# TensorE's expert loop with eight experts a turn in place of two

## The reference

```
logits = ht @ w_router + b_router
top_val, top_idx = lax.top_k(logits, 4)
gates = softmax(top_val)
# for each expert e and the tokens routed to it:
gu = x @ w_gate_up[e] + b_gate_up[e]            # 1024 -> 2048
gate = minimum(gu[:, :1024], 7.0); up = clip(gu[:, 1024:], -7.0, 7.0)
act = gate * sigmoid(1.702 * gate) * (up + 1)
y = act @ w_down[e] + b_down[e]                 # 1024 -> 1024, times the gate, summed per token
```

## Time and profile before

| what | value |
|---|---|
| median of 3 runs | 1282.84 us (1281.08 to 1282.91) |
| the profiled execution, its own time | 1281.37 us |
| its span, first to last instruction | 1279.6 us |
| PE busy | 1082.8 us (85%) |
| moved from memory | 457 MB, 357 GB/s over the span |
| mean granted TensorE clock | 0.911 of full speed |

### The profile page before, as it was taken

How to read it: one execution, slowest core, us unless ns; L and a number is a source line. 1 busy time by engine, 2 the same in 40 slices (tenths; PEclk the granted TensorE clock), 3 DMA queues, 4 the chain that set the end, 5 groups by cost and what they waited for, 6 DMA issues and landing times.

```text
span 1279.6 us, 28615 instructions
## 1 busy us (share of the span) xinstructions
PE 1082.8 (85%) x11083; PEld 516.1 (40%) x11084; DVE 306.7 (24%) x816; ACT 198.4 (16%) x444; POOL 111.9 (9%) x216
## 2 busy tenths in 40 slices
PE   3988999979997667766999999996769799969997
PEld 1776877735442111112444444441113244414443
DVE  0245344448221000001221122210001012212112
ACT  2330123332110000000111111110001011101112
POOL 8100002023010000000000010000000000000000
PEclk9998999989998786777999999997779799979999
DMA  9646334797999999999999989999999999999765
GB/s 349 227 164 225 106 130 173 284 303 271 386 422 422 422 422 422 422 422 422 422 422 422 422 344 423 422 422 422 422 422 422 422 422 422 422 422 422 308 265 212
DMA packets 81280, 457.27 MB, mean 357 GB/s; under 512 B 7054, under 2 KB 8176, under 8 KB 31936
## 3 DMA queue, kind: packets, MB, share of 16 engines
q1 hardware_dynamic: 74704, 417.91, 80.5%
q10 hardware_dynamic: 4976, 33.10, 6.3%
q0 software_dynamic: 1568, 5.80, 1.5%
HBM read 455.72 MB, written 1.07 MB: 357 GB/s over the span
## 4 chain that ended last, share of the span: by engine, by line
PE 48%; SPq 20%; DMA 18%; DVE 8%; issue 3%; ACT 2%; ACTq 1%; DVEq 0%
PE bank L1935 17%; SPq L366 15%; DMA raw<-in_w_gate_up 10%; PE bank L1948 9%; PE bank L1497 7%; DMA dn<-in_w_down 5%; SPq L370 4%; PE bank L1908 2%; DMA odd<-in_w_gate_up 2%; PE bank L1820 2%; PE bank L1957 2%; DMA raw<-in_w_ada 1%; DVE aT L1392 1%; PE bank L1462 1%; DVE gated L1377 1%
## 5 line engine op out<-in xcount | busy, mean ns | idle before, releaser
L1935 PE MATMUL bank<-raw,xT 128*32 128x512 f32 x1600 | 219.8, 680 | 82.3 <-DMA raw<-in_w_gate_up 70.3
L1935 PE MATMUL bank<-odd,xT 128*32 128x512 f32 x1664 | 213.2, 652 | 40.2 <-DMA odd<-in_w_gate_up 40.2
L1377 DVE TENSOR_TENSOR gated<-bank,bias_i 128x256 f32<-128x256 f32 x51 | 21.6, 424 | 614.4 <-PE bank L1957 614.4
L1935 PEld LDWEIGHTS bank<-raw,xT 128*32 128x32 f32 x1600 | 49.7, 115 | 237.1 <-DMA raw<-in_w_gate_up 142.2
L842 ACT ACTIVATE evg<-bank 128x512 f32<-128x512 f32 x51 | 30.5, 597 | 739.6 <-PE bank L1935 739.6
L580 POOL TENSOR_TENSOR gatehot<-onehot,gates 128x128 f32<-128x128 f32 x102 | 54.9, 557 | 881.2 <-PE bank L1924 869.5
L1935 PEld LDWEIGHTS bank<-odd,xT 128*32 128x32 f32 x1664 | 54.9, 113 | 181.8 <-issue 93.8
L1948 PE MATMUL bank<-raw,aT 128*32 128x256 f32 x2016 | 119.7, 380 | 9.4 <-DVE aT L1392 6.3
L1497 PE MATMUL bank<-hT,raw 128*128 128x256 f32 (+1 forms) x496 | 115.5, 392 | 2.2 <-ACT hT L633 2.2
L1497 PEld LDWEIGHTS bank<-hT,raw 128*128 128x128 f32 (+1 forms) x496 | 94.2, 193 | 21.3 <-issue 4.1
L1948 PEld LDWEIGHTS bank<-raw,aT 128*32 128x32 f32 x2016 | 62.4, 110 | 59.9 <-DVE aT L1392 16.3
(11 more groups left out here) (404 smaller groups left out, 852.3 us busy)
## 6 DMA issues: line engine op xcount, KB each, us to landing
raw<-in_w_gate_up SPq DMA_DIRECT2D x128, 1024.0 KB, 28.6
odd<-in_w_gate_up SPq DMA_DIRECT2D x128, 1024.0 KB, 26.5
raw<-in_w_down SPq DMA_DIRECT2D x49, 1024.0 KB, 27.3
dn<-in_w_down SPq DMA_DIRECT2D x48, 1024.0 KB, 28.7
raw<-in_w_down ACTq DMA_DIRECT2D x31, 1024.0 KB, 9.0
raw<-in_w_ada SPq DMA_DIRECT2D x12, 2048.0 KB, 9.1
raw<-in_w_in SPq DMA_DIRECT2D x7, 2048.0 KB, 12.8
raw<-in_w_out SPq DMA_DIRECT2D x2, 2048.0 KB, 9.2
```

The source lines that it names most:

```text
L1377: body.step("gate", tt(gated[:, :, :, :], turned[:, :, 0:2, :], bias_i[:, :, 0:2].unsqueeze(3).to_broadcast([P, 4, 2, CAP]), ALU.add))
L1935: g = mm(bank[0][j * CAP:(j + 1) * CAP, :], xT[:, u % 2, u // 2, :], gu_slab(u, p)[:, j * NC:(j + 1) * NC], start=u == 0, stop=u == KT - 1)
```

## The change

The outer loop has 4 turns in place of 16, and its body holds the code of eight experts in place of two. Parity and count of an expert are now worked out from its place n in the turn.

```diff
             pe.wait_ge(S("items_ready"), 4)
-            with pe.Fori(0, NE // 2) as q:
-                after = pe.value_load(first_item[0:1, bass.ds(2 * q, 1)], min_val=0, max_val=NI)
-                for p in range(2):
-                    e, first = 2 * q + p, after
+            with pe.Fori(0, NE // 8) as r:
+                after = pe.value_load(first_item[0:1, bass.ds(8 * r, 1)], min_val=0, max_val=NI)
+                for n in range(8):
+                    p, q = n % 2, 4 * r + n // 2
+                    e, first = 8 * r + n, after
                     after = pe.value_load(first_item[0:1, bass.ds(e + 1, 1)], min_val=0, max_val=NI)
                     with pe.Fori(first, after) as i:
```

## The result

The changed kernel takes 1291.74 us (median of 4 runs, 1289.89 to 1292.24) against 1282.53 for the kernel before (four runs, one more than in the table of the time before): ratio 1.0079, 95% interval 1.0063 to 1.0094. It is 9.2 us slower. The forecast was 1283.9 with a range up to 1290.5, so the time lies outside. In the profiled execution the span is 1290.3 us against 1279.6, 10.7 us more.

What follows compares the result with a forecast made beforehand. Transfers bound the kernel to 603 us and from 760 to 1180, TensorE between and at the end. -3.5 + 1.1 + 2.2 + 1.2 = +1.0 us gave 1282.4 profiled, 1283.9 as median; range 1278.8 to 1290.5.

Steps and rivals of the forecast that it cites:

- What bounds the kernel, and which edges count: Expert stage: transfers bound most, TensorE 603 to 758 us and the end; removed edges at experts 12, 14, 30 save 3.5 us.
- The code is fetched again in each turn: TensorE's outer loop: 2,800 instructions do not stay, so each turn fetches its 11 to 13 packets again; 65 to 75 packets.
- Hidden at experts 8 and 24, not at 16, with 1.3 us of margin: Three remaining turn edges: slab waits hide the stall at 8 and 24; at 16 it opens a 1.2 us transfer hole.
- I take 2.5: Jump back at the remaining turn edges: TensorE waits 2.5 us for a code packet, opening a 1.2 us hole at expert 16.
- rival 3: Jump at expert 16: a 5 us stall opens the hole by 3.7 us; +3.5 us in sum, 1286.3; chance 0.13.
- The packets on the DMA engines: 1.1 + 2.2 us, spread over 16: Full transfer stretches: refetched code delays the busiest engine 1.1 us a packet; 1.1 us in the first, 2.2 in the second.
- rival 2: Full transfer stretches: code packets share few DMA engines; +4.3 us, 1287.1 with eight, +9.8, 1292.6 with four; chance 0.27.

Runs made afterwards that it cites:

- the carried register: Two kernels, four and two experts a turn, next expert's first item number kept in a register instead of read; against the kernel before: 1279.27 and 1278.25 us.
- six a turn: Against the changed kernel, six experts in the loop body for 30 experts, the last two behind the loop: 1292.02 us, ratio 1.0084.
- moving the edges: Against the changed kernel, experts 0 and 1 before the loop and six behind, so turn edges stand at experts 10 and 18: 1283.49 us.
- sixteen a turn: Against the changed kernel, sixteen experts in the loop body, leaving one jump back, in front of expert 16: 1290.75 us, ratio 1.0065.

## Why the prediction was wrong

- *What bounds the kernel, and which edges count.* Right. The PE stretch lost 2.3 us for experts 12 and 14, and the end 1.2 us for expert 30. The removed edges in the long stretch gave nothing: it takes 425.5 us with two and with four experts a turn, and 425.4 us with the shorter edges of the carried register.
- *The code is fetched again in each turn.* Right: 69 packets, 65 to 75 foretold; six a turn shows that the limit lies between 1,400 and 2,100 instructions.
- *Hidden at experts 8 and 24, not at 16, with 1.3 us of margin.* Right: moving the edges showed that the place decides, and sixteen a turn that expert 16 is all of it.
- *"I take 2.5" for the stall.* This step failed. The jump was mis-sized. The edge idle grew by 7.29 - 1.12 = 6.2 us, beyond the 5 us of rival 3. A transfer's 1.9 us was no stand-in for a missed jump. The code packet itself is 1.1 us of it: the packet's record starts at 803.02, 3.9 us after the branch began to wait, and the branch ended 1.4 us after it. What fills the other 5 us no row names.
- *Left out altogether:* the clock behind the stall. 7.3 us of idle brought the granted clock to 0.51, and the next gate-up cost 9.46 - 7.07 = 2.4 us more. So TensorE was 8.6 us late at expert 16 against the 2.5 taken; less the 1.3 us of margin, that makes a hole of 7.3 us. The long stretch shows 7.1 us, against the 1.2 forecast.
- *The packets on the DMA engines: 1.1 + 2.2 us, spread over 16.* The mechanism was right, the size was off in the second term: 4.4 us, three packets on the busiest of about eight engines at some 1.5 us each in place of two at 1.1. That is rival 2 with its eight engines, which had 4.4 for this term; the equal figure is luck, since it took four packets at 1.1 us. The first stretch cost 1.0 us, close to the 1.1, but this is one pair of profiles: it takes 297.0 to 298.7 us in the five kernels that fetch 2 to 5 code packets in it and 298.6 to 300.2 in the seven others (15 to 17), so the term is some 1.3 us and not known to better than half a microsecond.
- The rivals 2 and 3 were priced one at a time, at +4.3 and +3.5. Both held at once, and rival 3 at twice its price. Put together with the measured sizes: -3.5 + 1.0 + 4.4 + 7.1 = +9.0, against 9.2 in the medians.

## What to carry to other kernels

When a loop body grows, count its instructions against what the trace shows to stay, and look at the queue that carries code: a body that fits fetches nothing after its first turn, one that doesn't pays twice, at the jump and on the DMA engines that carry data. A stall is worth what its place makes of it: ask how many microseconds of transfers are queued there, since the same 7 us of idle cost nothing at experts 8, 10, 18 and 24, 7 us at expert 16, and nearly 9 us, slow matmuls included, at expert 12. And when two dear cases have different causes, price them together as well as one by one.

## What the runs showed of the hardware

- A jump of TensorE's sequencer to code that was not kept left PE idle for 6.9 to 7.6 us in the kernels without the hint, against 1.1 us with the code kept. TensorE kept a loop of about 1,400 instructions and not one of about 2,100 (both counts are estimates from 350 for an expert).
- After 7.3 us of idle at expert 16 the granted clock was 0.51, the 1.2 GHz level, for about 5 us, and 64 matmuls took 9.46 us in place of 7.07.
- The DMA engines do not end together when code was fetched: about half of them go on, for 1.6 us after 8 packets and for 3 to 4.5 us after the 24 of the changed kernel's long stretch (20 of these begin in the second hole or behind it). From this the delay is estimated at some 1.5 us a packet, more than the 1.1 us of the packet itself. It stays until the queue runs dry.
- A branch hint at the top of the turn took one of three stalls down to 1.42 us and left 6.23 and 7.05 us at the two others. Why is open.
